# Stick-breaking weights transposed by VectorE and a DRAM bounce instead of TensorE

## The chip, the cores and the metric

The kernel runs on one core of one Trainium2 chip. The metric is the device time of one execution in microseconds. A profiled execution gives a page of summaries and a trace of every instruction; the engines are TensorE (PE in the profile, its weight loads PEld), VectorE (DVE), ScalarE (ACT), GpSimd (POOL) and SyncE (SP), which here only issues DMAs.

## What is computed

A two-layer trunk over 512 tokens of width 2048: a recurrent layer, then keys and values computed once, then an attention layer of the stick-breaking kind with 12 heads of 128, each layer with a memory branch beside it. What matters here is the attention of the second layer, for each head:

```python
mask = key_pos[None, :] < q_pos[:, None]
z = jnp.einsum('bhqd,bhkd->bhqk', q_blk, kh).astype(jnp.float32) * scale
log_beta = jax.nn.log_sigmoid(z)
log_keep = jnp.where(mask, jax.nn.log_sigmoid(-z), 0.0)
later = lax.cumsum(log_keep, axis=3, reverse=True) - log_keep
w = jnp.where(mask, jnp.exp(log_beta + later), 0.0)
return jnp.einsum('bhqk,bhkd->bhqd', w.astype(vh.dtype), vh)
```

The kernel computes the weight w as sigmoid(z) times a running product of sigmoid(-z), taken from the right. Its rows are queries and its columns are keys. The last product sums over keys, so TensorE needs w with the keys on the partitions: w has to be transposed.

## The kernel before

Every float32 product is made of three TensorE passes with operands split into a high and a low part (`three_passes`, lines 2126 to 2128). ScalarE rounds the high part, VectorE subtracts it to get the low part.

The second layer's input projection is done slab by slab. A slab (G, j) is 512 rows of 512 columns of `w_in_b`: SP loads it into `w_raw` (`load_slab`, L453, one semaphore wait and one DMA), ScalarE and VectorE split it into `w_hi` and `w_lo` (`split`, `split_next`: in slab j they split slab j + 1), TensorE multiplies it in four quarters t of 12 matmuls (`slab`, L2132). All of these buffers are double: the split of slab j + 1 waits for the end of slab j - 1, the load of slab j for the split of slab j - 2.

The stick-breaking heads are woven into these slabs. The loop over i takes three turns (`NPAIR`), each turn eight slabs and four heads h; head n = 4 i + h has an even and an odd slab. TensorE's queue is in order, and `hooks` say ahead of which quarter of a slab the attention work stands:

- `stick_scores` (L2456): four score tiles of 256, 128, 384 and 512 columns (`Z_ORDER`) into the PSUM tensor `aux`. Head 0's stand ahead of quarter 1 of its even slab, those of head h + 1 behind the values of head h.
- `stick_transposed` (L2466): ten 128x128 transposes into `aux`, ahead of quarter 0 of the odd slab (quarter 1 for head 0). They wait for `w_ready`.
- `stick_values` (L2476): twelve matmuls, ahead of quarter 2 of the odd slab (quarter 3 for head 0). They wait for `wt_low`.

ScalarE's program (L1205) runs: in the odd slab, wait for `wt_done`, copy the transposed weights from `aux` to `wt_hi`, then the split of the next slab; in the even slab the split of the next slab, then eight sigmoids (L1222, L1223), then the load of the next head's keys and values (`load_kv`). VectorE's (L1950) runs: in the odd slab the low part `wt_lo` (L1960), the split, gates or products of the slab's outputs in some slots (L1514, L1985, L1986), and the copy or product of the head's output behind `o_done` (L1993 to L1999); in the even slab the split, then for each of four tiles two masks, a scan and a product (L1970 to L1977), the last of which counts `w_ready`. The sigmoids and products lie in `keep` and `beta`.

GpSimd's queue carries, all through this stage, DMAs that add quarters of the output projection's weights in DRAM (`move`, L618; `weight_sums` in the profile). They have a semaphore of their own for each of four sets.

Of the kernel before, what the change touches and what calls it, by code (L numbers as in the profile page):

```python
# [19 lines left out]
P = 128  # L20
T = 512
# [3 lines left out]
C = 512  # L25
NT = T // P
# [3 lines left out]
NB = DR // P  # L30
# [31 lines left out]

WT_WIDTH = (512, 512, 256)
Z_ORDER = ((1, 3, 0), (0, 2, 384), (2, 2, 0), (3, 1, 0))

# [44 lines left out]
def trunk(nc, x, x_t, mem, mem_t, gain_cols, chan_cols, w_mem_kv, w_in_a, w_rec_gate, w_in_gate,  # L110
# [23 lines left out]
    def value_weights(n):  # L134
# [6 lines left out]
        return v_sums[k:k + P, at:at + VC]  # L141

    kv_dram = nc.dram_tensor("kv_scratch", [NB, P, 4, T], F32, kind="Internal").ap()

    with ExitStack() as ctx:
# [63 lines left out]
        wt_hi = split_at("wt_hi", [P, 1280], 2)  # L209
        wt_lo = split_at("wt_lo", [P, 1280], 2, 1280)  # L210
        ot = work[:, XR + 2048 * 2 + 2560:XR + 2048 * 2 + 3584].rearrange("p (b t) -> p b t", b=2)
        q_hi = split_at("q_hi", [P, 4, T], 6)
# [184 lines left out]
        w_ready = sem("w_ready")  # L397
        wt_done = sem("wt_done")
        wt_high = sem("wt_high")
# [30 lines left out]
        q22_loaded = [sem(f"q22_loaded{n}") for n in range(2)]  # L430
        sums_made = [sem(f"sums_made{n}") for n in range(4)]
        sum_ready = sem("sum_ready")
# [15 lines left out]
        def _(sp):  # L448
# [9 lines left out]
            def load_fill(f, src):  # L458
                sp.wait_ge(fill_lo, 4 * (f - 1))
                sp.dma_start(f_raw[:, f % 2], src).then_inc(f_loaded[f % 2], 16)  # L460

            def load_in(w, G0):

                def group(G, col):
                    for j in range(4):
                        load_slab(G, j, w[:, bass.ds(col, C)])
                for j in range(4):
                    if G0 == G_B and j < 2:
                        sp.wait_ge(v_lo, (V_TILES - 2, V_TILES)[j])
                    load_slab(G0, j, w[:, 0:C])  # L470
                    if G0 == G_A and j == 0:
                        load_fill(F_X + 3, x_tv[3])
                    if G0 == G_A and j < 2:
                        sp.dma_start(x_nat[:, 2 + j, :], x_v[:, 2 + j, :]).then_inc(nat_loaded[1], 16)
                with sp.Fori(0, NPAIR - 1) as i:
                    group(2 * i + (G0 + 1), C * i + DR)
                    group(2 * i + (G0 + 2), C * i + C)
                for q in range(2 * NPAIR - 1, 2 * NPAIR + 2):
                    group(G0 + q, in_column(q))
# [59 lines left out]
            def load_out(s, y):  # L539
# [10 lines left out]
                load_quad(y, q_22[s][0], KQ, 4, HALF, q22_loaded[0])  # L550
                sp.wait_ge(sums_made[2 * s], 16 * 32)
                load_proj(s, 2)
# [8 lines left out]
                for u in range(6, 14):  # L561
                    load_proj(s, u)
                sp.wait_ge(sums_made[2 * s + 1], 16 * 32)
                for u in range(14, N_PROJ):
# [38 lines left out]
        def _(pool):  # L603
# [13 lines left out]

            def move(n, dst, src, op):  # L618
                for r in range(4):
                    rows = slice(2 * P * r, 2 * P * r + 2 * P)  # L620
                    pool.dma_start(dst[rows], src[rows], accum_op=op).then_inc(sums_made[n], 16)

# [29 lines left out]
            for n in range(4):  # L652
                b11, b12, b21, b22, t1, t2, t3, t4 = weights(n // 2, n % 2)
                if n == 2:
# [10 lines left out]
                    for m in range(4):  # L665
                        store_value(m)
                move(n, t1, b11, ALU.bypass)
                move(n, t3, b12, ALU.bypass)
                pool.wait_ge(sums_made[n], 16 * 8)
                move(n, t1, b12, ALU.add)  # L670
                move(n, t3, b22, ALU.add)
                pool.wait_ge(sums_made[n], 16 * 16)
                move(n, t2, t1, ALU.bypass)
                pool.wait_ge(sums_made[n], 16 * 20)
                move(n, t2, b22, ALU.add)
                pool.wait_ge(sums_made[n], 16 * 24)
                move(n, t4, t2, ALU.bypass)
                pool.wait_ge(sums_made[n], 16 * 28)
                move(n, t4, b21, ALU.add)


        @blk.scalar
        def _(act):
# [521 lines left out]
            with act.Fori(0, NPAIR) as i:  # L1205
                for q in range(2):
                    G = 2 * i + (G_B + 1 + q)
                    for j in range(4):
                        h, second = (4 * q + j) // 2, j % 2
                        n = 4 * i + h  # L1210
                        if second:
                            act.wait_ge(wt_done, n + 1)
                            for b, w in enumerate(WT_WIDTH):
                                nc.scalar.activation(wt_hi[:, 512 * b:512 * b + w], aux[:, 1 + b, 0:w], ACT.Copy
                                                     ).then_inc(wt_high, 1)
                        split_next(G, j)
                        if not second:
# [11 lines left out]
                            if h < 3:  # L1229
                                load_kv(n + 1, (h + 1) % 2)  # L1230
                            else:

                                load_kv((4 * i + 4) % NB, 0)
                        if 4 * q + j == 4:
                            gate_sigmoid(2 * i + (G_B + 1))
# [76 lines left out]
        def _(dve):  # L1312
# [637 lines left out]
            with dve.Fori(0, NPAIR) as i:  # L1950
                ch.enter(i, PER_B)
                for q in range(2):
                    G = 2 * i + (G_B + 1 + q)
                    for j in range(4):
                        h, second, slot = (4 * q + j) // 2, j % 2, 4 * q + j
                        n = 4 * i + h
                        if second:
                            for b, w in enumerate(WT_WIDTH):
                                dve.wait_ge(wt_high, 3 * n + b + 1)
                                V.tensor_tensor(wt_lo[:, 512 * b:512 * b + w], aux[:, 1 + b, 0:w],  # L1960
                                                wt_hi[:, 512 * b:512 * b + w].bitcast(F32), ALU.subtract
                                                ).then_inc(wt_low, 1)
                        split_next(G, j)
                        if not second:
                            for m, (t, _, _) in enumerate(Z_ORDER):
# [10 lines left out]
                                ch.wait(a3)  # L1976
                                V.tensor_tensor(b[:, 0:w - 1], b[:, 0:w - 1], k[:, 1:w], ALU.mult).then_inc(w_ready, 1)  # L1977
                        if slot == 3:
                            dve.wait_ge(y_stored, 16 * i + 64)
# [141 lines left out]
        def _(pe):  # L2121
# [343 lines left out]

            def stick_transposed(i, h):  # L2466
                pe.wait_ge(w_ready, 4 * (4 * i + h) + 4)
                for k in range(NT):
                    bank, at = ((1, 0), (2, 0), (3, 0), (2, 384))[k]
                    for t in range(k, NT):  # L2470
                        o = aux[:, bank, at + P * (t - k):at + P * (t - k) + P]
                        c = T - P * (t + 1) + P * k
                        last = TE.transpose(o, beta[:, t, c:c + P], ident[:])  # L2473
                last.then_inc(wt_done, 1)

            def stick_values(i, h):  # L2476
# [3 lines left out]
                for k, n in order:  # L2480
                    at = (0, 512, 1024, 896)[k]
                    v = kv[:, h % 2, (2, 2, 3)[n], P * k:P * k + P]
                    w = (wt_hi, wt_lo, wt_hi)[n][:, at:at + T - P * k]
                    last = TE.matmul(aux[:, 0, P * k:T], v, w, start=(k, n) == order[0], stop=(k, n) == order[-1])  # L2484
# [7 lines left out]
            with pe.Fori(0, NPAIR) as i:  # L2492
                for q in range(2):
                    for j in range(4):
# [4 lines left out]
                        else:  # L2499
                            late = 1 if h == 0 else 0  # L2500
                            hooks = {late: lambda: stick_transposed(i, h),
                                     late + 2: lambda: (stick_values(i, h), stick_scores(i, h + 1) if h < 3 else None)}
                        slab(2 * i + (G_B + 1 + q), j, "T", hooks)
# [46 lines left out]
```

## Time and profile before

| | us |
|---|---|
| median of 3 runs | 1468.64 (1468.19 to 1468.73) |
| span of the profiled execution | 1466.5 |
| TensorE busy | 1458.0 (99%) |
| VectorE busy | 997.5 (68%) |
| ScalarE busy | 716.3 (49%) |

The span is the time from the first to the last instruction of one profiled execution. The page gives busy time of each engine, the span in 40 slices (busy tenths, the clock that TensorE was granted, DMA), the chain of work that ended last, and the costliest groups of instructions. The trace gives each instruction's start and length; a "<-" in a row names what ended the idle time ahead of it. In the PE rows the lengths overlap, since matmuls are pipelined: the distance between starts is what one costs.

### The profile page before, as it was taken

Reading aid. Unit: us, or ns where it says so; the run is one execution under the profiler, and the core shown is the slowest. Engines: PE = TensorE matmul, PEld = TensorE weight load, DVE = VectorE, ACT = ScalarE, POOL = GpSimd, SP = SyncE. Lnnn points to the kernel's source line nnn. Section 1 sums busy time; section 2 is a strip of 40 time slices with the busy share of each in tenths; the row PEclk is TensorE's granted clock in tenths of the full one; section 3 lists DMA queues with packets and bytes.
Section 4 is the critical chain, followed back from the end, with each engine's and each line's share of the span. In section 5 each row is a group of like instructions: output and inputs, shape, how many; then the busy total and the mean of one; then the engine's idle time right before and its main releaser. Section 6 shows DMA issues by size and latency. Waiting matters only on the chain.

```text
span 1466.5 us, 18207 instructions
## 1 busy us (share of the span) xinstructions
PE 1458.0 (99%) x6842; PEld 1221.7 (83%) x6842; DVE 997.5 (68%) x1317; ACT 716.3 (49%) x1066; POOL 122.8 (8%) x184
## 2 busy tenths in 40 slices
PE   9999999999999999999999999999999999999998
PEld 7888888888888888888888888888888888888886
DVE  6775568465576896856579676556566566578987
ACT  6764544444544645763325654433333433455465
POOL 0001111111110000000010001111111011000000
PEclk9999999999999999999999999999999999999999
DMA  9877788777886987477989876687888888858853
GB/s 344 290 287 225 159 215 228 174 235 158 212 251 165 323 323 260 155 262 282 358 326 372 291 224 219 244 218 196 230 241 244 202 239 208 226 188 329 315 200 144
DMA packets 154189, 357.97 MB, mean 244 GB/s; under 512 B 7824, under 2 KB 23440, under 8 KB 150032
## 3 DMA queue, kind: packets, MB, share of 16 engines
q1 hardware_dynamic: 103824, 205.98, 40.3%
q0 software_dynamic: 29376, 102.77, 28.3%
q10 hardware_dynamic: 20928, 48.41, 9.0%
q8 instruction: 38, 0.62, 0.2%
q14 instruction: 23, 0.19, 0.0%
HBM read 310.99 MB, written 113.25 MB: 289 GB/s over the span
## 4 chain that ended last, share of the span: by engine, by line
PE 99%; DMA 0%; SPq 0%; ACT 0%; issue 0%; DVE 0%; ACTq 0%
PE main L2128 25%; PE main L2127 25%; PE main L2126 25%; PE aux L2127 6%; PE aux L2126 6%; PE aux L2128 6%; PE aux L2484 2%; PE aux L2473 1%; DMA w_raw<-in_w_mem_kv 0%; PE aux L2270 0%; PE main L2178 0%; PE aux L2178 0%; PE main L2199 0%; PE main L2202 0%; PE main L2205 0%; PE aux L2220 0%
## 5 line engine op out<-in xcount | busy, mean ns | idle before, releaser
L2126 PE MATMUL main<-act_hi,w_hi 128*128 128x512 f32 x1216 | 475.3, 391 | 0.0
L2127 PE MATMUL main<-act_lo,w_hi 128*128 128x512 f32 x1216 | 473.6, 389 | 0.0
L2128 PE MATMUL main<-act_hi,w_lo 128*128 128x512 f32 x1216 | 473.6, 389 | 0.0
L2128 PEld LDWEIGHTS main<-act_hi,w_lo 128*128 128x128 f32 x1216 | 228.3, 188 | 47.4
L2127 PEld LDWEIGHTS main<-act_lo,w_hi 128*128 128x128 f32 x1216 | 228.4, 188 | 46.7
L2126 PEld LDWEIGHTS main<-act_hi,w_hi 128*128 128x128 f32 x1216 | 228.4, 188 | 46.4
L1334 DVE SCALAR_TENSOR_TENSOR w_lo<-w_raw,gains,w_hi 128x512 fp32r<-128x512 f32 x180 | 123.3, 746 | 120.5 <-ACT w_hi L704 120.5
L704 ACT ACTIVATE w_hi<-w_raw,gains 128x512 fp32r<-128x512 f32 x180 | 115.4, 712 | 140.6 <-PE main L2128 121.9
L1325 DVE TENSOR_TENSOR w_lo<-w_raw,w_hi 128x1024 fp32r<-128x1024 f32 x88 | 104.1, 1222 | 105.2 <-ACT w_hi L697 105.0
L697 ACT ACTIVATE w_hi<-w_raw 128x1024 fp32r<-128x1024 f32 x88 | 88.5, 1057 | 169.5 <-PE main L2128 132.7
L2126 PE MATMUL main<-w_hi,act_hi 128*128 128x512 f32 (+1 forms) x432 | 163.5, 378 | 0.0
L2127 PE MATMUL main<-w_lo,act_hi 128*128 128x512 f32 (+1 forms) x432 | 163.4, 378 | 0.0
L2128 PE MATMUL main<-w_hi,act_lo 128*128 128x512 f32 (+1 forms) x432 | 163.1, 377 | 0.0
L2126 PE MATMUL aux<-w_hi,act_hi 128*128 128x512 f32 (+1 forms) x348 | 129.4, 372 | 0.0
L2127 PE MATMUL aux<-w_lo,act_hi 128*128 128x512 f32 (+1 forms) x348 | 129.2, 371 | 0.0
L2128 PE MATMUL aux<-w_hi,act_lo 128*128 128x512 f32 (+1 forms) x348 | 128.9, 370 | 0.0
L2126 PEld LDWEIGHTS main<-w_hi,act_hi 128*128 128x128 f32 x432 | 81.3, 188 | 15.6
L2128 PEld LDWEIGHTS main<-w_hi,act_lo 128*128 128x128 f32 x432 | 81.2, 188 | 15.2
L2127 PEld LDWEIGHTS main<-w_lo,act_hi 128*128 128x128 f32 x432 | 81.3, 188 | 14.8
L755 ACT ACTIVATE w_hi<-work 128x1024 fp32r<-128x1024 f32 x56 | 56.3, 1053 | 64.2 <-issue 53.7
L755 ACT ACTIVATE w_hi<-w_raw 128x1024 fp32r<-128x1024 f32 x56 | 56.2, 1051 | 57.3 <-issue 57.3
L1372 DVE TENSOR_TENSOR w_lo<-w_raw,w_hi 128x1024 fp32r<-128x1024 f32 x56 | 66.2, 1220 | 25.7 <-ACT w_hi L755 25.6
(321 smaller groups left out, 1861.4 us busy)
## 6 DMA issues: line engine op xcount, KB each, us to landing
w_raw<-in_w_in_a SPq DMA_DIRECT2D x32, 1024.0 KB, 6.7
w_raw<-in_w_in_b SPq DMA_DIRECT2D x32, 1024.0 KB, 7.9
weight_sums<-in_w_out_a POOLq DMA_DIRECT2D x48, 512.0 KB, 7.0
weight_sums<-in_w_out_b POOLq DMA_DIRECT2D x48, 512.0 KB, 7.2
weight_sums<-weight_sums POOLq DMA_DIRECT2D x32, 512.0 KB, 6.4
w_raw<-weight_sums SPq DMA_DIRECT2D x16, 1024.0 KB, 6.6
work<-weight_sums SPq DMA_DIRECT2D x16, 1024.0 KB, 7.5
w_raw<-in_w_mem_kv SPq DMA_DIRECT2D x13, 1024.0 KB, 5.2
```

The costliest lines, as they stand in the source:

```text
L697: nc.scalar.activation(w_hi[:, j % 2, k:k + 2, :], raw[:, k:k + 2, :], ACT.Copy).then_inc(hi_ready, 2)
L704: nc.scalar.activation(w_hi[:, j % 2, k, :], raw[:, k, :], ACT.Copy, scale=s).then_inc(hi_ready, 1)
L755: nc.scalar.activation(w_hi[:, u % 2, k:k + 2, :], proj_raw[RAW[u]][:, k:k + 2, :], ACT.Copy).then_inc(hi_ready, 2)
L1325: V.tensor_tensor(w_lo[:, j % 2, k:k + 2, :], w_raw[:, j % 2, k:k + 2, :], w_hi[:, j % 2, k:k + 2, :].bitcast(F32), ALU.subtract).then_inc ...
L1334: V.scalar_tensor_tensor(lo, raw[:, k, :], gain[:, KS * j + k:KS * j + k + 1], hi, ALU.mult, ALU.subtract).then_inc(lo_ready, 1)
L1372: V.tensor_tensor(w_lo[:, u % 2, k:k + 2, :], proj_raw[RAW[u]][:, k:k + 2, :], w_hi[:, u % 2, k:k + 2, :].bitcast(F32), ALU.subtract).then ...
L2126: TE.matmul(o, a[0], b[0], start=first, stop=False)
L2127: TE.matmul(o, a[0], b[1], start=False, stop=False)
L2128: return TE.matmul(o, a[1], b[0], start=False, stop=final)
L2473: last = TE.transpose(o, beta[:, t, c:c + P], ident[:])
L2484: last = TE.matmul(aux[:, 0, P * k:T], v, w, start=(k, n) == order[0], stop=(k, n) == order[-1])
```

## The change

The ten transposes of a head leave TensorE. Instead VectorE transposes the 32x32 blocks of the weights, each for itself, in four instructions for each head, into `turned` (which lies over `keep`). SP stores `turned` to DRAM (`turn_scratch`, 128 rows of 1280 numbers), waits for the landing, and loads it back in four DMAs, 32 partitions each, so that the blocks come to lie on the right partitions, into `wt_lo`. ScalarE copies `wt_hi` from there and VectorE subtracts in place. The value matmuls read their moving operand in pieces of 32 numbers (`turned_back`). In the even slabs of heads 1 to 3 the sigmoids, masks and turns stand ahead of the next slab's split; head 0 keeps its order. SP's loop of slabs is written out, and the turn of head n stands ahead of the load of the slab that comes three behind the head's even slab. The four semaphores of the weight sums become one.

```diff
+    turn_dram = nc.dram_tensor("turn_scratch", [4, 32, 4, 320], F32, kind="Internal").ap()
...
+        turned = block(0)[:, 0:1280]
+
+        def turn_blocks(k):
+
+            at = XR + 2048 + 384 + 512 * k
+            src = work[:, at:at + 384 * (NT - k)].rearrange("p (t x) -> p t x", x=384)[:, :, 0:P]
+            dst = turned.rearrange("p (c n j) -> p n c j", c=4, j=32)[:, TURN_AT[k]:TURN_AT[k] + NT - k]
+            return dst, src.rearrange("p t (c i) -> p t c i", i=32)
+
+        def turned_back(w, k):
+
+            return w[:].rearrange("p (r n j) -> p n r j", r=4, j=32)[:, TURN_AT[k]:TURN_AT[k] + NT - k]
...
+            def turn_weights(n):
+
+                sp.wait_ge(wt_turned, 4 * n + 4)
+                sp.dma_start(turn_dram.rearrange("r i c m -> (r i) (c m)"), turned).then_inc(wt_stored, 16)
+                sp.wait_ge(wt_stored, 16 * n + 16)
+                for c in range(4):
+                    sp.dma_start(wt_lo[32 * c:32 * c + 32, :].rearrange("p (r m) -> p r m", r=4).bitcast(F32),
+                                 turn_dram[:, :, c, :].rearrange("r i m -> i r m")).then_inc(wt_loaded, 16)
...
+                if G0 == G_B:
+                    for q in range(1, 2 * NPAIR + 2):
+                        for j in range(4):
+                            n, ahead = divmod(4 * q + j - 7, 2)
+                            if ahead == 0 and 0 <= n < NB:
+                                turn_weights(n)
+                            load_slab(G0 + q, j, w[:, in_column(q):in_column(q) + C])
+                    return
...
@@ ScalarE
                         if second:
-                            act.wait_ge(wt_done, n + 1)
+                            act.wait_ge(wt_loaded, 64 * n + 64)
                             for b, w in enumerate(WT_WIDTH):
-                                nc.scalar.activation(wt_hi[:, 512 * b:512 * b + w], aux[:, 1 + b, 0:w], ACT.Copy
+                                part = slice(512 * b, 512 * b + w)
+                                nc.scalar.activation(wt_hi[:, part], wt_lo[:, part].bitcast(F32), ACT.Copy
                                                      ).then_inc(wt_high, 1)
-                        split_next(G, j)
+                        if second or h == 0:
+                            split_next(G, j)
...
+                            if h:
+                                split_next(G, j)
...
@@ VectorE
-                        split_next(G, j)
+                        if second or h == 0:
+                            split_next(G, j)
...
+                            dve.wait_ge(w_ready, 4 * n + 4)
+                            for k in range(NT):
+                                V.transpose(*turn_blocks(k)).then_inc(wt_turned, 1)
+                            if h:
+                                split_next(G, j)
...
@@ TensorE
-            def stick_transposed(i, h):
-                pe.wait_ge(w_ready, 4 * (4 * i + h) + 4)
-                for k in range(NT):
...
-                last.then_inc(wt_done, 1)
...
-                    w = (wt_hi, wt_lo, wt_hi)[n][:, at:at + T - P * k]
+                    w = turned_back((wt_hi, wt_lo, wt_hi)[n], k)
...
-                            hooks = {late: lambda: stick_transposed(i, h),
-                                     late + 2: lambda: (stick_values(i, h), stick_scores(i, h + 1) if h < 3 else None)}
+                            hooks = {late + 2: lambda: (stick_values(i, h), stick_scores(i, h + 1) if h < 3 else None)}
```

## Rows read from the trace of the kernel before

**Rows 1.** The page's first part: busy us, share of the span, instructions.

```profile
span 1466.5 us, 18207 instructions
PE 1458.0 (99%) x6842; PEld 1221.7 (83%) x6842; DVE 997.5 (68%) x1317; ACT 716.3 (49%) x1066; POOL 122.8 (8%) x184
```

**Rows 2.** The page's 40 slices: TensorE's granted clock and the DMA engines, in tenths.

```profile
PEclk9999999999999999999999999999999999999999
DMA  9877788777886987477989876687888888858853
```

**Rows 3.** The page's chain that ended last, by engine.

```profile
PE 99%; DMA 0%; SPq 0%; ACT 0%; issue 0%; DVE 0%; ACTq 0%
```

**Rows 4.** Timeline of PE, head 0 of turn 2: start us, us, engine line operation.

```profile
1034.39 0.39 PE L2126 MATMUL main<-act_hi,w_hi 128*128 128x512 f32 x1
...
1037.11 0.28 PE L2126 MATMUL aux<-kv,q_hi 128*128 128x256 f32 x1
...
1049.93 1.25 PE L2473 MATMUL aux<-ident,work 128*128 128x128 f32 x10
...
1056.49 0.39 PE L2484 MATMUL aux<-wt_hi,kv 128*128 128x512 f32 x1
...
1058.39 0.28 PE L2126 MATMUL aux<-kv,q_hi 128*128 128x256 f32 x1
...
1058.62 0.28 PE L2128 MATMUL aux<-kv,q_lo 128*128 128x256 f32 x1
...
1060.30 0.39 PE L2126 MATMUL main<-act_hi,w_hi 128*128 128x512 f32 x1
```

**Rows 5.** Timeline of DVE in the same turn, heads 0, 1 and 2.

```profile
1041.27 0.29 DVE L1970 TENSOR_TENSOR work<-work,m_keep 128x128 f32<-128x128 f32 x1 [0.49 <-ACT work L1223]
...
1046.06 1.21 DVE L1974 TENSOR_TENSOR_SCAN work<-work 128x511 f32<-128x511 f32 x1
1047.31 0.69 DVE L1977 TENSOR_TENSOR work<-work 128x511 f32<-128x511 f32 x1
1051.85 1.62 DVE L1960 TENSOR_TENSOR wt_lo<-aux,wt_hi 128x512 fp32r<-128x512 f32 x3 [3.85 <-ACT wt_hi L1214]
...
1058.59 0.69 DVE L1993 COPY work<-aux 128x512 f32<-128x512 f32 x1 [2.60 <-PE aux L2484]
...
1089.96 0.69 DVE L1514 TENSOR_TENSOR work<-main,rstd_bc 128x512 f32<-128x512 f32 x1 [2.03 <-PE main L2128]
...
1106.63 2.28 DVE L1985 TENSOR_TENSOR work<-work 128x2048 f32<-128x2048 f32 x1
1108.95 1.23 DVE L1986 TENSOR_TENSOR work<-work 128x1024 f32<-128x1024 f32 x1
```

**Rows 6.** Timeline of ACT, the same head 0: first sigmoid, copies of the transposed weights.

```profile
1040.57 0.38 ACT L1222 ACTIVATE work<-aux 128x256 f32<-128x256 f32 x1
...
1051.22 1.09 ACT L1214 ACTIVATE wt_hi<-aux 128x512 fp32r<-128x512 f32 x2 [7.89 <-PE aux L2473]
```

**Rows 7.** The page's group of VectorE's split: busy us, mean ns, idle before.

```profile
L1325 DVE TENSOR_TENSOR w_lo<-w_raw,w_hi 128x1024 fp32r<-128x1024 f32 x88 | 104.1, 1222 | 105.2 <-ACT w_hi L697 105.0
```

**Rows 8.** DMA issues at the kernel's end: count, KB each, median us to landing.

```profile
out<-work SPq DMA_DIRECT2D x6, 512.0 KB, 3.0
out<-work SPq DMA_DIRECT2D x2, 256.0 KB, 2.6
```

**Rows 9.** One stretch of 27 us, a head's: PE, PEld, DVE, ACT, POOL busy, PEclk, DMA share, GB/s.

```profile
1028.00:1055.00 27.00, 27.00 (x132) 22.82 (x132) 16.68 (x30) 12.99 (x21) 2.68 (x3) 1.00 0.82 235
```

**Rows 10.** The store of a turn's outputs, 1 MB, line 862, 900 to 1300 us: issue ns, landing.

```profile
L862 ACTq DMA_DIRECT2D y_scratch<-work x3: 418/427/428, 1030.0 to 1243.8; - x3
...
DMA to landing us min/median/max: 9.9/10.8/11.3
```

**Rows 11.** The load of a head's keys and values, 1 MB, line 1069, the same stretch.

```profile
L1069 ACTq DMA_DIRECT2D kv<-kv_scratch x13: 344/345/419, 917.0 to 1224.4; - x13
...
DMA to landing us min/median/max: 4.9/6.9/9.3
```

More of the change, by code:

```diff
@@ L63 @@
 WT_WIDTH = (512, 512, 256)
+TURN_AT = (0, 4, 7, 9)
 Z_ORDER = ((1, 3, 0), (0, 2, 384), (2, 2, 0), (3, 1, 0))
@@ L397, in trunk @@
         w_ready = sem("w_ready")
-        wt_done = sem("wt_done")
+        wt_turned = sem("wt_turned")
+        wt_stored = sem("wt_stored")
+        wt_loaded = sem("wt_loaded")
         wt_high = sem("wt_high")
@@ L430, in trunk @@
         q22_loaded = [sem(f"q22_loaded{n}") for n in range(2)]
-        sums_made = [sem(f"sums_made{n}") for n in range(4)]
+        sums_made = sem("sums_made")
         sum_ready = sem("sum_ready")
@@ L550, in load_out @@
                 load_quad(y, q_22[s][0], KQ, 4, HALF, q22_loaded[0])
-                sp.wait_ge(sums_made[2 * s], 16 * 32)
+                sp.wait_ge(sums_made, 16 * 32 * (2 * s + 1))
                 load_proj(s, 2)
@@ L562, in load_out @@
                     load_proj(s, u)
-                sp.wait_ge(sums_made[2 * s + 1], 16 * 32)
+                sp.wait_ge(sums_made, 16 * 32 * (2 * s + 2))
                 for u in range(14, N_PROJ):
@@ L616, in _, with move @@
                                     pattern=[[-1, P]], channel_multiplier=1).then_inc(const_ready, 1)
-            def move(n, dst, src, op):
+            def move(dst, src, op):
                 for r in range(4):
                     rows = slice(2 * P * r, 2 * P * r + 2 * P)
-                    pool.dma_start(dst[rows], src[rows], accum_op=op).then_inc(sums_made[n], 16)
+                    pool.dma_start(dst[rows], src[rows], accum_op=op).then_inc(sums_made, 16)
             def store_ht(c):
@@ L666, in _ @@
                         store_value(m)
[L667 to L679, printed above, removed]
+                if n:
+                    pool.wait_ge(sums_made, 16 * 32 * n)
+                move(t1, b11, ALU.bypass)
+                move(t3, b12, ALU.bypass)
+                pool.wait_ge(sums_made, 16 * (32 * n + 8))
+                move(t1, b12, ALU.add)
+                move(t3, b22, ALU.add)
+                pool.wait_ge(sums_made, 16 * (32 * n + 16))
+                move(t2, t1, ALU.bypass)
+                pool.wait_ge(sums_made, 16 * (32 * n + 20))
+                move(t2, b22, ALU.add)
+                pool.wait_ge(sums_made, 16 * (32 * n + 24))
+                move(t4, t2, ALU.bypass)
+                pool.wait_ge(sums_made, 16 * (32 * n + 28))
+                move(t4, b21, ALU.add)
         @blk.scalar
@@ L1959, in _ @@
                                 dve.wait_ge(wt_high, 3 * n + b + 1)
-                                V.tensor_tensor(wt_lo[:, 512 * b:512 * b + w], aux[:, 1 + b, 0:w],
-                                                wt_hi[:, 512 * b:512 * b + w].bitcast(F32), ALU.subtract
-                                                ).then_inc(wt_low, 1)
-                        split_next(G, j)
+                                part = slice(512 * b, 512 * b + w)
+                                V.tensor_tensor(wt_lo[:, part], wt_lo[:, part].bitcast(F32),
+                                                wt_hi[:, part].bitcast(F32), ALU.subtract).then_inc(wt_low, 1)
+                        if second or h == 0:
+                            split_next(G, j)
                         if not second:
@@ L2464, in stick_scores @@
                                  (kv[:, h % 2, 0, 0:w], kv[:, h % 2, 1, 0:w])).then_inc(z_done, 1)
-            def stick_transposed(i, h):
-                pe.wait_ge(w_ready, 4 * (4 * i + h) + 4)
-                for k in range(NT):
[L2469 to L2473, printed above, removed]
-                last.then_inc(wt_done, 1)
             def stick_values(i, h):
@@ L2480, in stick_values @@
                 for k, n in order:
-                    at = (0, 512, 1024, 896)[k]
                     v = kv[:, h % 2, (2, 2, 3)[n], P * k:P * k + P]
-                    w = (wt_hi, wt_lo, wt_hi)[n][:, at:at + T - P * k]
+                    w = turned_back((wt_hi, wt_lo, wt_hi)[n], k)
                     last = TE.matmul(aux[:, 0, P * k:T], v, w, start=(k, n) == order[0], stop=(k, n) == order[-1])
```

## The prediction

> **What bounds the kernel now.** I read the page's busy times first, then its clock and DMA tenths, then the chain that ended last. TensorE is busy for 1458.0 of 1466.5 us [rows 1], at a granted clock of 9 tenths or more in all 40 slices, 2.4 GHz [rows 2], and it holds 99% of the chain [rows 3]. So a microsecond taken off TensorE comes off the total, and one in which TensorE waits is added to it, while the other engines' own time costs nothing until TensorE waits for it. The change sits in one stage, the stick-breaking loop (about 927 to 1245 us): 12 heads, in three turns of four. The PE timeline of one head [rows 4] gives the sizes. Twelve matmuls of a slab's quarter go from 1034.39 to 1037.11, so the pitch is 0.2267 us, a quarter 2.72 and a slab 10.88. The values take 58.39 - 56.49 = 1.90, the scores 60.30 - 58.39 = 1.91. From the first transpose to the first value matmul it is 6.56 us with 24 slab matmuls (5.44) between, so a head's ten transposes cost 1.12.
>
> **What is removed.** 12 heads x 1.12 = 13.4 us of TensorE time, all on the path. Nothing else goes from TensorE, and each `stick_values` stays at its quarter of the slab. If nothing new waits, the profiled 1466.5 becomes 1453.1; the median of the runs, 1468.64, is 2.1 above the profiled span, and I add that: 1455.2.
>
> **What is added is a longer chain from scores to values.** Before, it was sigmoids, masks, transposes, ScalarE's copy, VectorE's low part. Now four VectorE turns, a 640 KB store to DRAM, the wait for its landing and four loads of 160 KB stand between the masks and the copy. I ask, head by head, how much time TensorE's own work leaves for store plus load (call it x). V is the start of a head's values, E the start of the slab that holds head 0's scores.
>
> The parts: the masks of a head take 6.73 us, from 1041.27 to 1047.31 + 0.69 [rows 5]. The turns of 512, 384, 256 and 128 elements are not in the trace: a plain VectorE operation on 511 elements takes 0.69, a scan on 511 takes 1.21 [rows 5], so 1280 elements lie between 1.75 and 3.1 us; I take 1.8, since a turn reads one operand and recurs on nothing. Copy and low part take 51.85 + 1.62 - 51.22 = 2.25 [rows 5, 6].
>
> - Head 0 (split stays ahead of the sigmoids): its masks end at E + 13.6 (1048.00 - 1034.39), turned at E + 15.4. Values are due after 2.72 + 1.91 + 8.16 in the first slab and three quarters (8.16) of the second, E + 20.95. Less the 2.25: **3.2 us** are left for x.
> - Head 1: the first score tile ends at 1058.62 + 0.28, V + 2.4 [rows 4]; 0.7 from a sigmoid's start to the mask [rows 5, 6] gives masks from V + 3.2 to 9.9 (VectorE's copy of the last output, V + 2.1 to 2.8, is over [rows 5]), turned at 11.75. Due at V + 1.90 + 1.91 + 2.72 + 10.88 + 5.44 = 22.85: **8.7** left.
> - Head 2: VectorE first does the gate's last bank, which waits for the end of the slab, V + 9.25; with its 0.2 wait and 0.69 [rows 5] the masks run from 10.15 to 16.9, turned at 18.7. Due at V + 25.57: **4.5** left. The split moved behind the turn ends 2.4 us later (two pieces of 1.22 [rows 7]), at 21.1; the next slab's second half is wanted at V + 20.13 + 1.36 = 21.5, so it just fits.
> - Head 3: low part, split (to V + 2.5), products of 2.28 and 1.23 and the output of 0.7 [rows 5] hold VectorE to V + 6.6; turned at 15.15; due at 25.57: **8.1** left.
>
> In the kernel before, head 1 to 3's masks began only after the next split and were just ready for the transposes; moving them ahead of it is what buys the 8.7, 4.5 and 8.1. It costs ScalarE and VectorE nothing else, since the split waits for the slab's end in any case.
>
> **x itself.** No store or load of this shape is in the trace. Store: with queues nearly empty, 256 KB land in 2.6 and 512 KB in 3.0 us [rows 8], so 640 KB in about 3.2 and the part that doesn't grow is about 2.2. In this stage GpSimd's queue keeps transfers running all the while (DMA share 0.82 of a head's stretch [rows 9]), and the only store there, 1 MB of outputs, lands in 9.9 to 11.3, median 10.8 [rows 10]; scaled above 2.2 to 640 KB that is 2.2 + 0.625 x 8.6 = 7.6. Load: 1 MB of keys and values lands in 4.9 to 9.3 [rows 11], which scales to 3.9 to 6.6; four issues of some 0.4 each, one behind the other [rows 10, 11], may add up to 1.2, so 3.9 to 7.8. The store is nearest to the one store of the stage but has larger pieces, so I take 4.8, under the middle; the load is nearest to the keys' median of 6.9, which scales to 5.1, and SP and ACT queues are quiet at that moment: I take 4.9. x = 9.7, ends 7.1 and 15.4.
>
> **The sum.** Waits of TensorE: 9.7 less 3.2, 8.7, 4.5, 8.1 is 6.5 + 1.0 + 5.2 + 1.6 = 14.3 for a turn of four, three turns: 42.9. Less 13.4: +29.5. TensorE's clock after a wait of 5 or 6 us is in no row, for it never idles in this stage (27.00 busy of 27 [rows 9]). From below a wait costs nothing more; from above values and scores (3.81 at 2.4 GHz) run at the lower level, 1.2 GHz, for 3.8 more. I take the middle, 1.9, for the six long waits: 11.4. 1468.6 + 29.5 + 11.4 = **1509.5 us**. The Trainium skill, page "TensorE: Matmul & The Clock Gate", Part 1, says that the throttled clock is the default and that activity releases it; by that the term would be nearer its upper end, 1521, and no run here shows it yet.
>
> **Costs taken as nothing.** SP waits at the store with the load of slab 3 + 2n (n the head) queued behind it: it starts some 10 us later than before, but its split comes a whole slab and a wait after that, 10 us or more away. VectorE's 1.8 us more for a head lie in a stage where it is busy 16.7 of 27 us [rows 9]. ScalarE waits for the loads ahead of the odd slab's split, but that split has until the slab's end, 9 us behind the values. The one semaphore for all sums makes GpSimd wait out one more landing between two sets of sums, and nobody waits for these before the output projection.
>
> **Rivals.**
> 1. *The bounce fits* (0.09): the other side. Its place is the wait ahead of `stick_values` in heads 0 and 2. Saved and lost are equal where (x - 3.2) + (x - 4.5) = 13.4 / 3, x = 6.1; at 5 it is 1.8 + 0.5 = 2.3 a turn, 1455.2 + 6.9 = 1462, and with x under 3.2 it is 1455. For it speaks that the store's pieces are large and the four loads start one after the other without a wait between; against it that the store alone takes 3.2 on quiet queues and the loads cannot begin before it has landed.
> 2. *Quiet-queue transfers* (0.14): x = 3.2 + 3.9 = 7.1, waits 3.9 + 0 + 2.6 + 0 = 6.5 a turn, 19.5 - 13.4 = +6.1, 1475, with little clock lost. The 4.9 of some key loads, with GpSimd's queue running, speak for it; the 9.9 of the output store against it. The Trainium skill, page "DMA: Bandwidth & Descriptors", Anatomy of one DMA, fits a transfer as 2.0 us plus bytes at 436 GB/s; the estimate by it is 3.5 for each way, x = 7.0 and the same 1475. Key loads of 6.9 in the middle, against 4.4 by that fit, speak against it here.
> 3. *Contended transfers* (0.13): x = 13, waits 9.8 + 4.3 + 8.5 + 4.9 = 27.5 a turn, 82.5 - 13.4 = +69, and with 1.9 for each of 12 waits 1560.
> 4. *The value matmuls read pieces of 32 elements more slowly* (0.06): their moving operand becomes strided, and no matmul of the trace reads so. At half the rate 12 x 1.9 = 23 us more, 1532 with the forecast's waits.
>
> The forecast has the remaining 0.58. A rule against the change stands in the Trainium skill, page "VectorE: DVE Perf Modes", Rules for kernel authors: a 128x128 transposition belongs on TensorE if PSUM will do as its destination, as it did here. It gives no price for this case; the rows give TensorE's as 1.12 a head.
>
> **Range and chances.** What a measurement of this kernel can tell from no change is about 0.2%, 2.9 us: 1465.7 to 1471.6. Faster 0.07 (most of rival 1), same 0.04 (x near 6.1, the rest of rival 1 and an edge of rival 2), slower 0.89. The range goes from 1471, between rivals 1 and 2, to 1560, rival 3's own time.
>
> **What would show it.** Right: idle time of TensorE ahead of the value matmuls, longest for heads 0 and 2 of each turn, 5 to 7 us, with the low part of the turned weights named as what it waited for and behind it the DMA landings; no waits elsewhere; slabs at a pitch of 0.2267. Store and loads landing in about 5 us each confirm x. A granted clock below 1.0 in the stretch behind a long wait confirms the clock term. Wrong if the value matmuls start without idle time, if heads 1 and 3 wait as long as 0 and 2 (then a step I placed under cover is on the path), or if the waits stand ahead of slab matmuls, where a late split would put them.

## The result, and the profile after

The changed kernel takes 1563.17 us (median of 4 runs, 1559.98 to 1579.85) beside 1468.58 for the kernel before on the same chip; the ratio is 1.066, with a 95% interval of 1.061 to 1.071. The forecast was slower, at 1509.5, with a range that ended at 1560. The profiled execution is the shortest of the four, 1559.98 with a span of 1557.8; the sums below are made against it and the span before, 1466.5 [rows 1]: 91.3 us more.

The page after: busy times, the slices of TensorE's clock and of the DMA engines, and the chain that ended last, by engine and then by line.

```profile
span 1557.8 us, 18022 instructions
PE 1467.9 (94%) x6722; PEld 1227.2 (79%) x6722; DVE 1016.3 (65%) x1365; ACT 719.7 (46%) x1066; POOL 122.4 (8%) x184
PE   9999999999999999999999996769779796999998
PEclk9999999999999999999999997889889898999999
DMA  9777787777797974779898758888878887539854
PE 78%; DMA 10%; DVE 5%; issue 3%; ACT 2%; SPq 1%; DVEq 0%; ACTq 0%
PE main L2172 19%; PE main L2173 19%; PE main L2174 19%; PE aux L2172 6%; PE aux L2173 6%; PE aux L2174 6%; DMA wt_lo<-turn_scratch 5%; DMA turn_scratch<-work 5%; PE aux L2519 2%; DVE work L2015 2%; SPq L485 1%; DVE work L2021 1%; ACT w_hi L733 1%; DVE work L2011 1%; ACT wt_hi L1251 1%
```

TensorE no longer holds 99% of the chain [rows 3]. It is idle only in the slices of the stick-breaking stage (slices 24 to 33 of 0 to 39, and at the very end), the granted clock is lower in the same slices and nowhere else, and 10% of the chain is the two halves of the bounce. The waits that end TensorE's idle time, and who waited for the two transfers (total us, times, longest):

```profile
PE aux L2519 <- DVE wt_lo L2001: 80.7, 10, 14.0
ACT wt_hi L1251 <- DMA wt_lo<-turn_scratch: 209.4, 12, 24.0
SPq L485 <- DMA turn_scratch<-work: 68.7, 12, 8.8
```

Nearly all the idle time that TensorE gained, 80.7 us, stands ahead of the value matmuls (line 2519), in 10 of 12 heads; no slab matmul of the stage waits. Head 0 of the second turn shows one wait whole (timelines of VectorE, SP, ScalarE and TensorE, in order of time):

```profile
1087.55 1.69 DVE L2021 STREAM_TRANSPOSE work<-work 128x512 f32<-128x512 f32 x4
1089.27 0.34 SPq L482 DMA_DIRECT2D turn_scratch<-work  x1
1093.09 2.25 SPq L485 DMA_DIRECT2D wt_lo<-turn_scratch  x4
1094.06 0.39 PE L2174 MATMUL main<-act_hi,w_lo 128*128 128x512 f32 x1
1101.53 1.45 ACT L1251 ACTIVATE wt_hi<-wt_lo 128x512 fp32r<-128x512 f32 x3 [18.70 <-DMA wt_lo<-turn_scratch]
1103.88 0.79 PE L2519 MATMUL aux<-wt_hi,kv 128*128 128x512 f32 x1 [9.43 <-DVE wt_lo L2001]
1104.47 0.63 PE L2519 MATMUL aux<-wt_lo,kv 128*128 128x512 f32 x1
1104.89 1.16 PE L2519 MATMUL aux<-wt_hi,kv 128*128 128x512 f32 x3
...
1107.56 0.41 PE L2172 MATMUL aux<-kv,q_hi 128*128 128x256 f32 x1
```

The store is issued as soon as the turns are done, its landing releases the loads 3.8 us later, and ScalarE's copy starts 8.4 us after that: x, the time for store plus load, is 12.3 here. Two more things stand in these rows. The third value matmul starts 0.42 behind the second, both of 512 columns, where a matmul of 512 columns goes at 0.2267 in [rows 4], and the values take 1107.56 - 1103.88 = 3.68 us in place of 1.90. The windows of that stretch give the granted clock (the columns are those of [rows 9]):

```profile
1096.00:1103.00 7.00, 0.00 (x0) 0.00 (x0) 0.81 (x2) 1.47 (x4) 0.90 (x1) 0.64 1.05 275
1104.00:1108.00 4.00, 4.00 (x15) 3.71 (x16) 2.56 (x3) 0.88 (x1) 0.91 (x1) 0.50 0.37 66
1108.50:1112.50 4.00, 4.00 (x21) 3.40 (x21) 3.34 (x11) 2.75 (x8) 0.00 (x0) 1.00 0.99 275
```

0.50 is the lower level, 1.2 GHz: the clock fell while TensorE waited (a mean of 0.64 in the first row, in which no matmul ran), stayed there through the values, and was back at 2.4 GHz within a microsecond of the scores' start.

The same reading of all twelve heads, from the timelines (us; store is from its issue to the first load's issue, load from there to ScalarE's copy, x their sum):

| head | store | load | x | idle of TensorE |
|---|---|---|---|---|
| 0 of the three turns | 7.5, 3.8, 2.9 | 9.9, 8.4, 8.5 | 17.4, 12.3, 11.4 | 14.0, 9.4, 8.3 |
| 1 | 8.5, 8.4, 4.5 | 9.5, 6.6, 7.7 | 18.0, 15.0, 12.2 | 8.4, 6.0, 2.5 |
| 2 | 7.9, 4.1, 9.2 | 9.2, 4.9, 9.7 | 17.1, 9.0, 18.9 | 12.2, 4.2, 14.0 |
| 3 | 4.8, 4.4, 7.0 | 6.3, 6.3, 5.2 | 11.1, 10.7, 12.2 | 0, 0, 1.7 |
| mean | 6.1 | 7.7 | 13.8 | 80.7 in all |

The account of the 91.3 us: -13.4 for the transposes, +80.7 of waits, and 24.0 that are neither, 2.4 for each of the ten waits. Behind the shortest of them, 1.7 us, the matmuls kept their pitch, so it is nearer 2.7 for each of nine. These 24.0 lie in TensorE's busy time: 1467.9 is 23.3 above the 1458.0 - 13.4 that the same matmuls would take at the pitch of before.

### The profile page after: what moved, and what is told of

Same layout as the page of the kernel before. It is cut to its first block, busy times and chain, and to the rows that moved or that the text cites. A ratio compares the mean times of both kernels' runs of the same rounds, so it can differ in the third digit from the quotient of the medians.

```text
span 1557.8 us, 18022 instructions
## 1 busy us (share of the span) xinstructions
PE 1467.9 (94%) x6722; PEld 1227.2 (79%) x6722; DVE 1016.3 (65%) x1365; ACT 719.7 (46%) x1066; POOL 122.4 (8%) x184
## 4 chain that ended last, share of the span: by engine, by line
PE 78%; DMA 10%; DVE 5%; issue 3%; ACT 2%; SPq 1%; DVEq 0%; ACTq 0%
PE main L2172 19%; PE main L2173 19%; PE main L2174 19%; PE aux L2172 6%; PE aux L2173 6%; PE aux L2174 6%; DMA wt_lo<-turn_scratch 5%; DMA turn_scratch<-work 5%; PE aux L2519 2%; DVE work L2015 2%; SPq L485 1%; DVE work L2021 1%; ACT w_hi L733 1%; DVE work L2011 1%; ACT wt_hi L1251 1%
## 5 line engine op out<-in xcount | busy, mean ns | idle before, releaser
L1365 DVE TENSOR_TENSOR w_lo<-w_raw,w_hi 128x1024 fp32r<-128x1024 f32 x88 | 103.7, 1217 | 66.5 <-ACT w_hi L733 66.3
L733 ACT ACTIVATE w_hi<-w_raw 128x1024 fp32r<-128x1024 f32 x88 | 88.1, 1048 | 101.9 <-PE main L2174 65.0
L2001 DVE TENSOR_TENSOR wt_lo<-wt_lo,wt_hi 128x512 fp32r<-128x512 f32 (+1 forms) x36 | 19.6, 599 | 153.4 <-ACT wt_hi L1251 153.4
L1251 ACT ACTIVATE wt_hi<-wt_lo 128x512 fp32r<-128x512 f32 (+1 forms) x36 | 17.5, 548 | 209.4 <-DMA wt_lo<-turn_scratch 209.4
L2519 PE MATMUL aux<-wt_hi,kv 128*128 128x128 f32 (+2 forms) x96 | 35.0, 461 | 80.7 <-DVE wt_lo L2001 80.7
L2519 PEld LDWEIGHTS aux<-wt_hi,kv 128*128 128x128 f32 x96 | 25.9, 284 | 88.1 <-DVE wt_lo L2001 85.2
```

What stands on the lines that cost most here:

```text
L733: nc.scalar.activation(w_hi[:, j % 2, k:k + 2, :], raw[:, k:k + 2, :], ACT.Copy).then_inc(hi_ready, 2)
L1251: nc.scalar.activation(wt_hi[:, part], wt_lo[:, part].bitcast(F32), ACT.Copy).then_inc(wt_high, 1)
L1365: V.tensor_tensor(w_lo[:, j % 2, k:k + 2, :], w_raw[:, j % 2, k:k + 2, :], w_hi[:, j % 2, k:k + 2, :].bitcast(F32), ALU.subtract).then_inc ...
L2001: V.tensor_tensor(wt_lo[:, part], wt_lo[:, part].bitcast(F32), wt_hi[:, part].bitcast(F32), ALU.subtract).then_inc(wt_low, 1)
```

## The experiments

The theory after this reading: the order of the steps and the time that TensorE leaves for them were as forecast, x was set too low, because GpSimd's queue delays the store and the loads, and the lower clock behind each wait makes the rest. The rivals: the narrow loads are slow by themselves; the strided value matmuls are; the reorder itself costs; the 24 us are not the clock.

### The bounce left out

```diff
-                            if ahead == 0 and 0 <= n < NB:
-                                turn_weights(n)
...
-                            act.wait_ge(wt_loaded, 64 * n + 64)
+                            act.wait_ge(wt_turned, 4 * n + 4)
...
-                                nc.scalar.activation(wt_hi[:, part], wt_lo[:, part].bitcast(F32), ACT.Copy
+                                nc.scalar.activation(wt_hi[:, part], turned[:, part], ACT.Copy
...
-                                V.tensor_tensor(wt_lo[:, part], wt_lo[:, part].bitcast(F32),
+                                V.tensor_tensor(wt_lo[:, part], turned[:, part],
```

> The store to DRAM and the four loads are left out: ScalarE's copy and VectorE's low part read the turned blocks where VectorE left them, so the blocks lie on the wrong partitions and the attention's output is not the reference's. All else is as after the change. Theory (the bounce alone makes the waits, the value matmuls read pieces of 32 at full pitch): the transposes' 13.4 us come off and nothing waits, 1455 us. Rival (strided reading at half the rate): 23 us more, 1478. Rival (the moved split or the turns themselves are on the path): idle time of TensorE ahead of slab or value matmuls, above 1460.

1456.02 us (1454.95 to 1458.36), ratio 0.991 (0.990 to 0.993). The groups of value matmuls before, the same groups in this run, and TensorE's one wait inside the work:

```profile
L2484 PE MATMUL aux<-wt_hi,kv 128*128 128x128 f32 (+2 forms) x96 | 22.4, 320 | 0.0
L2484 PE MATMUL aux<-wt_lo,kv 128*128 128x512 f32 (+3 forms) x48 | 13.5, 322 | 0.0
...
L2517 PE MATMUL aux<-wt_hi,kv 128*128 128x128 f32 (+2 forms) x96 | 22.6, 322 | 0.0
L2517 PE MATMUL aux<-wt_lo,kv 128*128 128x512 f32 (+3 forms) x48 | 13.5, 322 | 0.0
PE aux L2170 <- DVE w_lo L1410: 3.0, 1, 3.0
```

The strided reading costs nothing: 22.6 and 13.5 us for these groups, where before 22.4 and 13.5. No wait is left in the stage. The 3.0 us are one late split in the output projection, behind a transfer of its weights, in this execution; 1466.5 - 13.4 + 3.0 = 1456.1 is the profiled span of 1456.2, and the spans of the three other runs, 1452.8 to 1453.9, are near the 1453.1 without it. So what the kernel after takes above some 1456 us comes with the bounce.

### The reorder alone, and the bounce without it

On the kernel before, heads 1 to 3 only get the new order:

```diff
-                        split_next(G, j)
+                        if second or h == 0:
+                            split_next(G, j)
...
+                            if h:
+                                split_next(G, j)
```

> The kernel before the change with one part of it alone: the sigmoids and masks of heads 1 to 3 stand ahead of the next slab's split; TensorE's transposes stay, and there is no bounce. Theory (the reorder moves only work that TensorE does not wait for): 1468.3 us, no change within 0.2%. Rival (head 2's split, moved behind masks that wait for a gate's last bank, comes late for its slab): up to 2 us a turn, 1470 to 1475.

1468.53 us, ratio 0.9999 (0.9990 to 1.0009): no change, as the theory had it. The same edit taken back in the kernel after:

> The kernel after the change with one part undone: in the even slabs of heads 1 to 3 the next slab's split stands ahead of the sigmoids, masks and turns again, on ScalarE and on VectorE. Theory (the reorder is what buys time for the bounce): the masks of heads 1 to 3 end 10.5 us into the even slab and are turned at 12.3, the values are due at 16.3, so 1.8 us are left for store and loads in place of 8.7, 4.5 and 8.1; with transfers of 13.8 us that is some 16 us of waits more for a turn of four heads, 1600 to 1625 us. Rival (the reorder is worth little, since the split waits for the slab's end in either order): 1560 to 1575.

1621.88 us (1614.86 to 1628.71), ratio 1.104 (1.100 to 1.108). TensorE waits 139.0 us, in all twelve heads:

```profile
PE aux L2513 <- DVE wt_lo L1998: 139.0, 12, 16.4
```

The reorder is worth nothing alone and 59 us with the bounce. The mean x of this run, read in the same way, is 13.8 again, and x less the wait leaves 3.4 for head 0, whose order is the same, and 1.5 to 1.9 for heads 1 to 3, where 1.8 was worked out. So what the order changes is the time that TensorE leaves in these heads, not engine time.

### GpSimd's sums left out

```diff
-        return (b11, b12, b21, b22, *(sums_dram[2 * s + n, m] for m in range(4)))
+        return (b11, b12, b21, b22, *(sums_dram[n, m] for m in range(4)))
...
+                if n >= 2:
+                    continue
```

> GpSimd's sums of the second output projection's weights are left out (the projection reads the first layer's sums, so its output is not the reference's); GpSimd's queue is silent in the stick-breaking stage. All else is as after the change. Theory (the bounce takes 13.8 us on average, not the 9.7 of the forecast, because GpSimd's queue shares the DMA engines): store and loads land in 3 to 4 us each, x falls to 7 to 8, waits to 7 to 9 us a turn of four heads, time to 1475 to 1490. Rival (the shape is slow by itself: four loads of 32 partitions, a DRAM write that has to land before they start): x stays above 11, time above 1530.

1489.62 us (1484.93 to 1494.77), ratio 1.013 (1.011 to 1.016). Landings of the store and of the loads from their issue (min, median, max), in the kernel after and then in this one, and TensorE's waits in this one:

```profile
DMA to landing us min/median/max: 2.9/5.9/9.2
DMA to landing us min/median/max: 2.7/5.2/8.5
```

```profile
DMA to landing us min/median/max: 2.9/2.9/3.6
DMA to landing us min/median/max: 2.5/3.1/4.1
PE aux L2521 <- DVE wt_lo L2003: 22.3, 6, 4.9
```

The DMA share of one stretch of 27 us, with the columns of [rows 9], where it was 0.82 before:

```profile
1028.00:1055.00 27.00, 27.00 (x128) 22.69 (x127) 17.72 (x31) 13.10 (x21) 0.00 (x0) 1.00 0.48 163
```

With GpSimd's queue silent the store takes 2.9 in nearly every head, the four loads 5.0 from the first issue to ScalarE's copy, x is 8.0 on average and 7.6 to 9.0 throughout. So 5.8 of the 13.8, and nearly all of their spread (9.0 to 18.9), are GpSimd's traffic. The six waits that are left are those of heads 0 and 2, 4.4 to 4.9 and 2.8 to 3.0 us; x less the wait gives the time that TensorE leaves, 3.4 and 4.9, where the forecast worked out 3.2 and 4.5. Still slower than the kernel before: the bounce does not fit on a quiet queue either.

### One wide load

```diff
-                for c in range(4):
-                    sp.dma_start(wt_lo[32 * c:32 * c + 32, :].rearrange("p (r m) -> p r m", r=4).bitcast(F32),
-                                 turn_dram[:, :, c, :].rearrange("r i m -> i r m")).then_inc(wt_loaded, 16)
+                sp.dma_start(wt_lo[:].bitcast(F32),
+                             turn_dram.rearrange("r i c m -> (r i) (c m)")).then_inc(wt_loaded, 16)
...
```

> The four loads of 32 partitions, with pieces of 1280 bytes, become one load of 128 partitions with pieces of 5120 bytes; the blocks are not moved between partitions, so the attention's output is not the reference's. GpSimd's sums run as in the kernel. Theory (the load's 7.7 us are its queueing among GpSimd's transfers; the shape costs only the three further issues, about 1.2 us): time falls by 5 to 20 us, to 1543 to 1558. Rival (narrow loads with short pieces are what is slow): the load lands in some 4 us, and the time falls by 30 us or more.

1534.10 us (1531.30 to 1540.28), ratio 1.046 (1.043 to 1.048): 29 us less than the kernel after, beyond the 5 to 20 that I gave the theory and just under the rival's 30. The load takes 6.4 in place of 7.7, about the three issues of the theory and not the rival's 4. But the store, which the edit doesn't touch, also took less, 5.2 in place of 6.1. To take GpSimd's traffic out of it, both edits together:

> Both edits of the two runs before: GpSimd's sums left out and one load of 128 partitions in place of four of 32 (output not the reference's). On a quiet queue it separates the load's shape from GpSimd's traffic. Theory (the shape costs only the three further issues): the load takes 3.5 to 4.0 in place of 5.0 us, the store stays at 2.9, x falls from 8.0 to 6.7, and the time from 1489.6 by 6 to 12 us to 1478 to 1484. Rival (narrow loads are slow by themselves, two or three us more): x below 6, waits only for head 0, time below 1475.

1482.29 us (1480.55 to 1483.75), ratio 1.009 (1.008 to 1.011). The store takes 2.9, the load 4.1, x 6.9 to 7.1 in all heads. So the narrow shape costs 0.9 us for each head, near its three further issues of some 0.4, and the time falls by 7 us, within what was expected. Why the store was quicker with the wide load beside GpSimd's traffic isn't settled; the heads fall at other points of GpSimd's sums in that run.

The Trainium skill, page "DMA: Bandwidth & Descriptors", Anatomy of one DMA, fits a transfer that GpSimd issues as 2.0 us plus its bytes at 436 GB/s; for 640 KB the estimate by it is 3.5 us each way. SP issues the two transfers here: their 2.9 and 4.1 agree with that in sum, the 13.8 beside GpSimd's traffic do not.

### The clock behind a wait

Extra matmuls fill part of the wait, so that TensorE is not idle for long. With GpSimd's queue silent, where the waits are steady:

```diff
+                pe.wait_ge(z_read, 4 * (4 * i + h) + 4)
+                for _ in range((16, 0, 10, 0)[h]):
+                    TE.matmul(aux[:, 1, :], ones_r[:], act_hi[:, 0, :], start=True, stop=True)
                 pe.wait_ge(wt_low, 3 * (4 * i + h) + 3)
...
```

> GpSimd's sums for the second output projection are left out as in the run before (output not the reference's), and TensorE does 16 extra matmuls (3.6 us) ahead of the wait of head 0 and 10 (2.3 us) ahead of that of head 2, less than the 4.4 to 4.9 and 2.8 to 3.0 us that it waited there. Theory (the lower clock behind a wait is a cost of its own, about 17 of the 26.6 us by which that run's span exceeds the one before the change): the granted clock stays at 0.99 or more and the time falls by 9 to 15 us, to 1475 to 1481. Rival (the clock is no cost of its own): 1488 to 1491.

1480.26 us (1479.27 to 1483.16), ratio 1.008 (1.007 to 1.010): 9.4 us less than with GpSimd's sums left out alone, with 78 matmuls more. One wait of head 0 without the filler, from the run on GpSimd's sums, and then with it, each with the values behind it (TensorE's timeline), and the mean clock of the run with it:

```profile
1068.19 0.79 PE L2521 MATMUL aux<-wt_hi,kv 128*128 128x512 f32 x1 [4.45 <-DVE wt_lo L2003]
1068.78 0.63 PE L2521 MATMUL aux<-wt_lo,kv 128*128 128x512 f32 x1
1069.21 1.16 PE L2521 MATMUL aux<-wt_hi,kv 128*128 128x512 f32 x3
```

```profile
1063.75 0.50 PE L2524 MATMUL aux<-wt_hi,kv 128*128 128x512 f32 x1 [1.09 <-DVE wt_lo L2003]
1064.09 0.40 PE L2524 MATMUL aux<-wt_lo,kv 128*128 128x512 f32 x1
1064.32 0.68 PE L2524 MATMUL aux<-wt_hi,kv 128*128 128x512 f32 x3
...
core 0: 1477.9 us, clock 0.999
```

The account without the filler: span 1493.1, 26.6 more than before, is -13.4 + 22.3 of waits + 17.7 that are neither. With it: 11.4 more is -13.4 + 4.9 of waits + 17.7 for the 78 matmuls + 2.2. So 15.5 of the 17.7, 2.6 for each of six waits, were the clock. That holds for the execution that was profiled, the longest of its four (1494.77 us; the others 1484.93 to 1492.24, at a higher mean clock). By the medians the same sum gives 9.7 us, 1.6 for each wait, if the waits were as long in the runs without a trace. In the kernel after itself, with 32, 16 and 24 extra matmuls:

> Ahead of the wait for the turned weights TensorE does 32, 16, 24 and 0 extra matmuls of 512 columns for heads 0 to 3 (7.3, 3.6, 5.4 and 0 us) into a PSUM bank that is free then. They fill idle time where the wait is longer and cost time where it is shorter. Theory (of the 91.3 us that the profiled run lost, 24 are the lower clock behind the waits): the granted clock stays nearer 1.0 and the time falls by 8 to 20 us, to 1543 to 1555. Rival (those 24 us are waits that the idle figures miss, or slower reading of the strided weights): no fall, 1560 or more.

1554.99 us (1552.34 to 1563.29), ratio 1.061 (1.058 to 1.064): 8 us less, at the low end. Waits of 31.4 us in all, up to 7.0, were left, and 16.6 of the former 24.0; the transfers vary too much from head to head for a filler of fixed length.

### Copies between groups of partitions in place of the bounce

Only the time from the turns to ScalarE's copy matters, so I replaced the store and the loads by sixteen copies of 32 partitions by 320 numbers, eight on each of two engines, into the buffer of the sigmoids, which is free by then. ScalarE's and VectorE's split into high and low parts read from there.

```diff
+        def quadrant_move(m):
+
+            r, c = m % 4, m // 4
+            return (block(1)[32 * c:32 * c + 32, 320 * r:320 * r + 320],
+                    turned[32 * r:32 * r + 32, 320 * c:320 * c + 320])
...
-                            if ahead == 0 and 0 <= n < NB:
-                                turn_weights(n)
...
-                            act.wait_ge(wt_loaded, 64 * n + 64)
+                            act.wait_ge(wt_turned, 4 * n + 4)
+                            for m in range(8):
+                                nc.scalar.activation(*quadrant_move(m), ACT.Copy).then_inc(wt_loaded, 1)
+                            act.wait_ge(wt_loaded, 16 * n + 16)
...
+                            dve.wait_ge(wt_turned, 4 * n + 4)
+                            for m in range(8, 16):
+                                V.tensor_copy(*quadrant_move(m)).then_inc(wt_loaded, 1)
```

> In place of the store and the loads, ScalarE and VectorE copy the sixteen groups of 32 partitions by 320 numbers from one group of partitions to another, eight each, into the sigmoids' buffer that is free by then. Nothing is left out. Theory (only the time from turn to copy matters, and 8 copies of about 0.4 us take 3.3 in place of 13.8): waits of 0.4 for head 0 and about 1 for head 2 of each turn, 1456 to 1461 us, faster than the kernel before. Rival (the copies cost more by going from one group of partitions to another, or push VectorE's splits onto the path): 1470 or more.

1460.01 us (1459.59 to 1460.41), ratio 0.994 (0.993 to 0.996): faster than the kernel before. The copies of the first head, on VectorE and ScalarE, ScalarE's copy for the split, and TensorE's waits in all heads:

```profile
942.68 2.93 DVE L2033 COPY work<-work 32x320 f32<-32x320 f32 x8
942.68 3.92 ACT L1254 ACTIVATE work<-work 32x320 f32<-32x320 f32 x8 [6.44 <-DVE work L2028]
946.64 1.46 ACT L1258 ACTIVATE wt_hi<-work 128x512 fp32r<-128x512 f32 x3
PE aux L2529 <- DVE wt_lo L2008: 2.4, 6, 0.6
```

From the end of the turns to the copy it is 4.0 us in head 0, ScalarE's eight copies end last, and TensorE waits 0.55 (4.0 against 3.2 or 3.4). In head 2 it is 5.1 us, because VectorE's copies stand behind its split there and end last, and TensorE waits 0.2 to 0.3. One more run gave ScalarE seven and VectorE nine:

> As the copies between groups of partitions, but seven on ScalarE and nine on VectorE. In that run ScalarE's eight took 3.9 us and VectorE's eight 2.9, and TensorE waited 2.4 us in all, 0.55 for head 0 and 0.2 for head 2. Theory (the waits go by the later of the two engines): ScalarE ends 0.5 us earlier, waits below 1.2 us in all, 1458.5 to 1460 us. Rival (what is left above the 1455.2 without waits is not these waits): 1460.

1459.52 us (1458.84 to 1462.17), ratio 0.994 (0.993 to 0.995). TensorE's waits, and head 2 of the first turn (VectorE's copies, ScalarE's copy for the split, the first value matmul):

```profile
PE aux L2529 <- DVE wt_lo L2008: 1.7, 3, 0.6
...
992.18 3.13 DVE L2033 COPY work<-work 32x320 f32<-32x320 f32 x9
995.34 1.46 ACT L1258 ACTIVATE wt_hi<-work 128x512 fp32r<-128x512 f32 x3 [1.97 <-DVE work L2033]
997.69 0.50 PE L2529 MATMUL aux<-wt_hi,kv 128*128 128x512 f32 x1 [0.57 <-DVE wt_lo L2008]
```

Head 0 no longer waits, but VectorE's ninth copy makes head 2's wait longer, some 0.6 in each turn, so the 1.7 us are more than the 1.2 expected. Whether 1459.5 differs from 1460.0 the runs cannot tell. Of the profiled span, 1456.6, some 1.8 us above 1466.5 - 13.4 are not these waits, and what they are stays open.

## Why the prediction was wrong in size

By its own steps. **What is removed** was right: 13.4 us, shown by the run without the bounce. **The chain and its budgets** were right: the turns took 1.69 us (1.8 forecast), and the times left for x came out at 3.4 for head 0 and 4.9 for head 2 with GpSimd's queue silent (3.2 and 4.5; the working's own numbers give 3.3, 8.85, 4.6 and 8.2, a sum of 24.9 in place of 24.5). Heads 1 and 3 had more than the 8.7 and 8.1: x less the wait is 9.0 to 9.7 for head 1 and 10.5 for head 3 of the last turn, and head 3 of the first did not wait with an x of 11.1. One source of this shows in the rows: the values and scores behind a wait run at half the pitch, and the time that they take longer is time for the next head's chain. In the run with 32, 16 and 24 extra matmuls, head 3 had 11.5 where the values of head 2 ahead of it ran at half the pitch (first turn), and 8.7 and 8.6 where they kept it. That is why a mean x of 13.8 gave 80.7 us of waits, where 4 x 13.8 - 24.5, three times, would be 92; most of the difference is in head 3.

**x was the mis-sized term, and the step that failed**: 9.7 forecast, 13.8 measured, inside the bounds of 7.1 and 15.4 but far from where I put it. I took the store at 4.8, under the middle of its bounds, for its large pieces; it measured 6.1 on average and up to 9.2, and no run shows a gain from the pieces. I took the load at 4.9; it measured 7.7. That 4.9 is under the 5.1 scaled from the keys' median and leaves out the issues of the four loads, which I had put at up to 1.2 and which measured 0.9. Its reason, that the queues are quiet at that moment, doesn't hold either: in the head shown SP issues a slab's load at 1095.38, right behind the four. What that load costs is not separated, but with it still there and GpSimd's queue silent the four loads take 5.0. What fills the DMA engines in this stage is to a large part GpSimd's queue (a share of 0.82 with it [rows 9] and 0.48 without, in the same stretch), and the run without it takes x to 8.0. In the profiled execution the error of the waits is 80.7 - 42.9 = 37.8 us and that of the clock 24.0 - 11.4 = 12.6, together 50.4 of the 50.5 by which its 1559.98 exceeds the forecast.

Rival 3, contended transfers, worked out 1560 from x = 13 and came within 3 us of the median, but I gave it 0.13 and ended the range at its own value, so the range left out half of it. Its closeness is partly luck: it lets all twelve heads wait, head 3 for 4.9 us, where ten did and head 3 waited once, for 1.7, and its x was 0.8 too low.

**The clock term** had the right mechanism and was too small, mostly by count: I charged 1.9 us to six waits, and there were ten, at 2.4 each; the runs with GpSimd's queue silent, with and without filler, show 1.6 to 2.6 for each of six. The Trainium skill, page "TensorE: Matmul & The Clock Gate", Part 1, says that the throttled clock is the default and that activity releases it; the 0.50 behind the waits agrees. The 1521 by that page lay nearer to the measured time, but with up to 3.8 us for each of six waits, where ten cost 2.4 each.

**Costs taken as nothing** held: no slab matmul waited for a split, SP's delayed weight loads were in time, and the strided reading of rival 4 is free. Rival 1's turning point also held from both sides: an x of 7.0 and of 8.0 is slower than before, the 4.0 to 5.1 of the copies faster, with 6.1 worked out between them.

## What to carry to other kernels

Work taken off the bound engine is a gain only if its substitute fits into the time that this engine leaves between producer and consumer: work out that time for each place in the program, then compare it with the transfer's duration beside the traffic that runs there, not alone. A round trip through DRAM is two landings in a row, and beside GpSimd's traffic the store took 2.9 to 9.2 us and the loads 4.9 to 9.9, so the middle of such bounds is no safe value. Where blocks only have to change partitions, engine copies kept the chain within 0.6 us of its budget.

## What the runs showed of the hardware

- Copies from one group of 32 partitions to another take 0.32 us on VectorE and 0.47 on ScalarE for 320 float32 columns (medians of 96 each).
- A store of 640 KB landed in 2.9 us with GpSimd's queue silent and in 2.9 to 9.2 beside it, by head.
- TensorE's clock was at 1.2 GHz behind the eight waits of 4.2 to 14.0 us in the kernel after; in the run without the bounce one wait of 3.0 us left the pitch unchanged (0.23 behind it), and with GpSimd's queue silent waits of 2.8 us were followed by half the pitch. In the run that also has the one wide load, one of three waits of 2.1 us was followed by half the pitch and two were not.
